# Norm statistics as full-width products with a stationary of ones, and the root and reciprocal on 512 columns

## The reference

```
def rmsnorm(x, g):
    xf = x.astype(jnp.float32)
    y = xf * lax.rsqrt(jnp.mean(xf * xf, axis=-1, keepdims=True) + EPS) * g.astype(jnp.float32)
    return y.astype(x.dtype)

def layer_norm(x, w, b, eps=LN_EPS):
    xf = x.astype(jnp.float32)
    mu = jnp.mean(xf, axis=-1, keepdims=True)
    var = jnp.mean(jnp.square(xf - mu), axis=-1, keepdims=True)
    y = (xf - mu) * lax.rsqrt(var + eps)
    return (y * w.astype(jnp.float32) + b.astype(jnp.float32)).astype(x.dtype)

def first_block(x, ...):
    u = rmsnorm(h, norm_mix_pre[l])
    z = u @ w_in[l]
    ...
    h = h + rmsnorm(m @ w_out[l], norm_mix_post[l])
    u2 = rmsnorm(h, norm_mlp_pre[l])
    a = jnp.square(jax.nn.relu(u2 @ w_up[l]))
    h = h + rmsnorm(a @ w_down[l], norm_mlp_post[l])

def second_block(x, c, ...):
    h = rms_norm(x, norm_mix_w[i]) * (1.0 + scale) + shift
    x = x + gate * mixer_sublayer(h, ...)
    h = rms_norm(x, norm_ffn_w[i]) * (1.0 + scale) + shift
    x = x + gate * ffn_sublayer(h, w_ffn_in[i], w_ffn_down[i])
    return rms_norm(x, final_norm_w)
```

## Time and profile before

| | us |
|---|---|
| median of three runs (lowest, highest) | 1763.21 (1762.67, 1766.19) |
| the profiled execution | 1764.47 |
| its span | 1762.7 |
| TensorE busy | 1714.2 (97%) |
| VectorE busy | 870.5 (49%) |
| ScalarE busy | 688.9 (39%) |
| GpSimd busy | 820.1 (47%) |

### The profile page before, as it was taken

The page is one execution under the profiler, slowest core; times in us unless marked ns, Lnnn a source line. Parts: engine busy times, 40 slices in busy tenths (PEclk is TensorE's granted clock), DMA queues, the critical chain, the costliest instruction groups (busy, mean ns, idle before and its releaser), DMA issues.

```text
span 1762.7 us, 22062 instructions
## 1 busy us (share of the span) xinstructions
PE 1714.2 (97%) x7994; PEld 1389.4 (79%) x7994; DVE 870.5 (49%) x1262; ACT 688.9 (39%) x933; POOL 820.1 (47%) x615
## 2 busy tenths in 40 slices
PE   7999999899999999899999999999999999999997
PEld 4777778678888888677888888778888788888886
DVE  4333464481817177588787878862544311101112
ACT  4333364421212123446465564684423322222231
POOL 4343354444546465443434434344455344664453
PEclk9999999899999999899999999999999899999998
DMA  4222222262534452142332232212223122332232
GB/s 180 72 72 73 93 75 93 81 228 109 195 139 178 155 178 96 51 143 96 107 109 95 95 119 95 96 67 101 94 74 115 59 98 101 128 120 95 95 120 95
DMA packets 30199, 193.26 MB, mean 110 GB/s; under 512 B 3360, under 2 KB 3360, under 8 KB 11328
## 3 DMA queue, kind: packets, MB, share of 16 engines
q1 hardware_dynamic: 23184, 158.89, 25.0%
q10 hardware_dynamic: 6960, 33.62, 5.7%
HBM read 190.34 MB, written 2.16 MB: 109 GB/s over the span
## 4 chain that ended last, share of the span: by engine, by line
PE 79%; issue 10%; POOL 7%; DVE 2%; ACT 2%; DMA 1%; POOLq 0%; DVEq 0%; SPq 0%; ACTq 0%
PE gemm_bank L465 19%; PE gemm_bank L458 19%; PE gemm_bank L459 18%; POOL w_lo L421 7%; PE gemm_bank L512 5%; PE gemm_bank L496 5%; PE gemm_bank L505 3%; PE gemm_bank L500 2%; PE aux_bank L815 1%; ACT w_hi L1000 1%; PE aux_bank L564 1%; PE aux_bank L820 1%; PE aux_bank L800 1%; DMA w_raw<-weights_dram 1%; PE aux_bank L590 1%
## 5 line engine op out<-in xcount | busy, mean ns | idle before, releaser
L421 POOL TENSOR_TENSOR w_lo<-w_raw,w_hi 128x512 fp32r<-128x512 f32 x588 | 795.0, 1383 | 911.8 <-ACT w_hi L1000 911.8
L458 PE MATMUL gemm_bank<-a_hi,w_hi 128*128 128x512 f32 x1216 | 486.3, 400 | 1.4 <-ACT w_hi L1000 1.4
L459 PE MATMUL gemm_bank<-a_lo,w_hi 128*128 128x512 f32 x1216 | 476.2, 392 | 0.0
L1000 ACT ACTIVATE w_hi<-w_raw 128x2048 fp32r<-128x2048 f32 x147 | 280.2, 1906 | 186.1 <-PE gemm_bank L465 138.8
L465 PE MATMUL gemm_bank<-a_hi,w_lo 128*128 128x512 f32 x1216 | 307.2, 395 | 2.7 <-POOL w_lo L421 2.7
L458 PEld LDWEIGHTS gemm_bank<-a_hi,w_hi 128*128 128x128 f32 x1216 | 229.8, 189 | 53.6 <-issue 4.8
L465 PEld LDWEIGHTS gemm_bank<-a_hi,w_lo 128*128 128x128 f32 x1216 | 226.6, 188 | 56.3 <-issue 5.5
L459 PEld LDWEIGHTS gemm_bank<-a_lo,w_hi 128*128 128x128 f32 x1216 | 229.8, 189 | 48.1 <-issue 1.9
L1788 DVE SCALAR_TENSOR_TENSOR aux_bank<-scratch,gcol,aux_bank 128x511 f32<-128x511 f32 (+15 forms) x240 | 165.9, 735 | 15.0 <-ACT aux_bank L1199 12.7
L458 PE MATMUL gemm_bank<-b_hi,w_hi 128*128 128x512 f32 x368 | 144.8, 394 | 0.0
L459 PE MATMUL gemm_bank<-b_lo,w_hi 128*128 128x512 f32 x368 | 143.4, 390 | 0.0
(11 more groups left out here) (327 smaller groups left out, 2099.6 us busy)
## 6 DMA issues: line engine op xcount, KB each, us to landing
w_raw<-weights_dram SPq DMA_DIRECT2D x147, 1024.0 KB, 4.7
arena<-ada_dram ACTq DMA_DIRECT2D x32, 768.0 KB, 4.3
acc<-cum_rows ACTq DMA_DIRECT2D x8, 512.0 KB, 3.8
...
```

Of the source, the lines that this page charges most:

```text
L421: ins = pool.tensor_tensor(wlo[s][:, w], raw[s][:, w], whi[s][:, w].bitcast(F32), ALU.subtract)
L458: pe.matmul(gemm_bank[bank][:, :], whi[slot][:, w], hi[:, k, :], start=(n == 0), stop=False)
L459: pe.matmul(gemm_bank[bank][:, :], whi[slot][:, w], lo[:, k, :], start=False, stop=False)
L1000: act.activation(whi[panel % 2][:, :], raw[panel % 2][:, :], ACT.Copy).then_inc(w_hi_ready, 1)
```

## The change

Five places get another form: the first norm, the residual of the first block, the convolution's layer norm (mean and variance), the norm before the FFN, and the final norm. The operands change roles. The 128x128 matrix of ones is stationary and the 128x512 sum moves, so that one product gives the sum over channels of every token, already repeated on all 128 partitions, as a 128x512 bank. `row_root` takes the root of the whole bank into `r_row`, `row_inverse` the reciprocal of all 512 columns into `aux[1]` (into `r_row` itself at the first norm). The spreading products and the copy of the first norm go; the mean is folded into a fused centering on VectorE.

At the residual, only seven squares are added on VectorE; the eighth is summed by a second product. The norms before the MLP and between the blocks, and the sums by groups of the scan's output, are as before.

```
 
+            def first_sums():
+
+                pe.wait_ge(sq_ready, KC)
+                pe.wait_ge(added[0], 6)
+                pe.matmul(aux[0][:, :], ones[:, :], sq[:, 1, :], start=True, stop=False)
+                pe.matmul(aux[0][:, :], ones[:, :], sq_acc, start=False, stop=True).then_inc(sum_done, 1)
...
                 if first:
-                    sums(0)
+                    first_sums()
                 tile_high(i, 1, 2, 4, 8, wide(2), a_hi, a_lo, first=True)
-                if first:
-                    spread(0)
                 tile_low(i, 1, 2, 4, wide(2), a_hi, first=True)
...
-            def sums_of_sum(steps, squares_made=None):
+            def row_sums(steps, squares_made):
 
                 pe.wait_ge(sq_sum_step, steps)
-                parts = [sq_sum]
-                if squares_made is not None:
-                    pe.wait_ge(ysq_ready, squares_made)
-                    parts.append(sq[:, 1, :])
-                for n, of in enumerate(parts):
-                    for j in range(QT):
-                        mm = pe.matmul(aux[0][:, j:j + 1], of[:, j * P:(j + 1) * P], ones[:, 0:1],
-                                       start=(n == 0 and j == 0), stop=(n == len(parts) - 1 and j == QT - 1),
-                                       skip_group_check=True)
-                mm.then_inc(sum_done, 1)
-
-            sums_of_sum(9)
-            spread(1)
+                pe.matmul(aux[0][:, :], ones[:, :], sq_sum, start=True, stop=False)
+                pe.wait_ge(ysq_ready, squares_made)
+                pe.matmul(aux[0][:, :], ones[:, :], sq[:, 1, :], start=False, stop=True).then_inc(sum_done, 1)
+
+            row_sums(8, 8)
...
-            def token_sums(parts, signal):
-                for n, of in enumerate(parts):
-                    for j in range(QT):
-                        mm = pe.matmul(aux[0][:, j:j + 1], of[:, j * P:(j + 1) * P], ones[:, 0:1],
-                                       start=(n == 0 and j == 0), stop=(n == len(parts) - 1 and j == QT - 1),
-                                       skip_group_check=True)
-                mm.then_inc(signal, 1)
-
             gate_tile(0)
             pe.wait_ge(u_sum_step, KC)
             pe.wait_ge(uc_ready, KC)
-            token_sums((u_sum,), mean_done)
-            gate_tile(1, (0,))
-            pe.wait_ge(mean_ready, 1)
-            for j in range(QT):
-                mm = pe.matmul(aux[1][:, j * P:(j + 1) * P], neg_mean[:, j:j + 1].to_broadcast([P, P]), ident[:, :],
-                               start=True, stop=True)
-            mm.then_inc(mean_spread, 1)
-            gate_tile(1, (1, 2))
+            pe.matmul(aux[1][:, :], ones[:, :], u_sum, start=True, stop=True).then_inc(mean_spread, 1)
+            gate_tile(1)
             gate_tile(2)
+            pe.wait_ge(ln_low_step, 3)
+            pe.matmul(aux[0][:, :], ones[:, :], ln_sq[:, 0, :], start=True, stop=False)
             pe.wait_ge(ln_sum_step, 3)
-            pe.wait_ge(ln_low_step, 3)
-            token_sums((ln_sq[:, 0, :], ln_sum), sum_done)
-            gate_tile(3, (0,))
-            spread(5)
-            gate_tile(3, (1, 2))
+            pe.matmul(aux[0][:, :], ones[:, :], ln_sum, start=False, stop=True).then_inc(sum_done, 1)
+            gate_tile(3)
...
-            spread(6)
+            row_sums(25, 24)
...
+            def row_root(n, e=0):
+                act.wait_ge(sum_done, n + 1)
+                act.activation(r_row, aux[0][:, :], ACT.Sqrt, bias=eps[:, e:e + 1], scale=1.0 / D).then_inc(root_ready, 1)
...
-            roots(0, sum_done, 1)
+            row_root(0)
...
-            roots(5, sum_done, 6, e=1)
+            row_root(5, e=1)
...
+            def row_inverse(n, dst):
+                dve.wait_ge(root_ready, n + 1)
+                dve.reciprocal(dst, r_row).then_inc(r_ready, 1)
+                dve.wait_ge(r_ready, n + 1)
+                dve.sem_inc(rinv_ready, 1)
+
             def normed_shifted(n, q, base, part):
 
-                inverse(n)
-                dve.wait_ge(r_ready, n + 1)
+                row_inverse(n, aux[1][:, :])
                 for k in range(KC):
                     dve.scalar_tensor_tensor(a_raw[:, k, :], h[:, k, :],
                                              gain2[:, KC * part + k:KC * part + k + 1], aux[1][:, :],
...
-                inverse(n)
-                dve.wait_ge(r_ready, n + 1)
+                row_inverse(n, aux[1][:, :])
                 dve.wait_ge(a_lo_ready, a_used)
...
-            root_row(0)
+            row_inverse(0, r_row)
+            dve.sem_inc(r_row_ready, 1)
...
             dve.memset(sq_sum, 0.0).then_inc(sq_sum_step, 1)
-            with dve.Fori(0, 2) as i:
-                for j in range(4):
-                    dve.wait_ge(ysq_ready, 4 * i + j + 1)
-                    dve.wait_ge(sq_sum_step, 4 * i + j + 1)
-                    dve.tensor_tensor(sq_sum, sq_sum, sq[:, j % 2, :], ALU.add).then_inc(sq_sum_step, 1)
+            for k in range(KC - 1):
+                dve.wait_ge(ysq_ready, k + 1)
+                dve.wait_ge(sq_sum_step, k + 1)
+                dve.tensor_tensor(sq_sum, sq_sum, sq[:, k % 2, :], ALU.add).then_inc(sq_sum_step, 1)
+            dve.wait_ge(sq_sum_step, KC)
+            dve.sem_inc(sq_sum_step, 1)
...
-            dve.wait_ge(mean_done, 1)
-            dve.tensor_scalar(neg_mean[:, :], aux[0][:, 0:QT], -1.0 / D, None, ALU.mult).then_inc(mean_ready, 1)
             dve.wait_ge(mean_spread, 1)
             for k in range(KC + 2):
                 if k < KC:
-                    dve.tensor_tensor(conv_u[:, k, :], conv_u[:, k, :], aux[1][:, :], ALU.add).then_inc(centered, 1)
+                    dve.scalar_tensor_tensor(conv_u[:, k, :], aux[1][:, :], -1.0 / D, conv_u[:, k, :],
+                                             ALU.mult, ALU.add).then_inc(centered, 1)
...
-            inverse(5)
-            dve.wait_ge(r_ready, 6)
             dve.wait_ge(centered, KC)
+            row_inverse(5, aux[1][:, :])
             dve.wait_ge(yz_ready, 4 * GROUPS)
...
-            inverse(7)
-            dve.wait_ge(r_ready, 8)
+            row_inverse(7, aux[1][:, :])
```

13 lines of the change are left out of this document (4 added, 9 removed).

## The result

The changed kernel takes 1765.82 us (median of 20 runs, 1764.52 to 1767.55), the kernel before 1761.94 in the same session (20 runs, 1760.46 to 1766.29). The ratio is 1.0018, with a 95% interval of 1.0012 to 1.0024: slower by 3.2 us, between 2.1 and 4.2. The forecast was +4.35 us and 1767.6. Direction and mechanism were right; the difference of the medians is 3.9. Of the 1.8 us by which the time itself is under the forecast, 1.3 belong to the starting point: the three runs shown of before had a median of 1763.21, the twenty of the comparison 1761.94.

What follows compares the result with a forecast made beforehand. TensorE, busy 97% of the span, was taken as the bound, with chain length deciding at the norms; -1.2 + 1.6 + 0 + 1.0 + 1.45 + 1.5 = +4.35 us gave 1767.6 us, range 1764.0 to 1771.0.

Steps and rivals of the forecast that it cites:

- What bounds the kernel: Whole kernel: TensorE is busy 97% of the span; at each changed norm only the length of the chain counts.
- The reciprocal: VectorE at all five places: 512 columns take 3.36 us, from the slope of narrower rows; +3.2 us in each chain.
- Rivals two: Five reciprocals: each is dearer, 3.82 us, adding 2.3 us to the sum, 1769.9 us; chance 0.12.
- three: Five reciprocals: 9.3 ns a column, up to 4.9 us each, adding 7.7 us, 1775.3 us; chance 0.06.
- four: Five reciprocals: divides overlap, 0.69 us each, so the change gains 7.9 us, 1755.3 us; chance 0.07.
- First norm: First norm: scores begin earlier, the long reciprocal being covered by the third tile; -1.2 us.
- Residual: Residual of the first block: sums end 0.75 us earlier, but the first scaled chunk comes later; +1.6 us.
- Layer norm: Convolution's layer norm: 0 us for the chain through ScalarE, +1.0 us because TensorE idles and its clock falls.
- FFN norm: Norm before the FFN: clock falls during the sums, scaling starts later; +1.45 us, +2.2 if the clock holds.
- final norm: Final norm: the same chain with nothing behind it, scaling starts later; +1.5 us, 2.2 with a warm clock.
- The sum: All five places together: +4.35 us, forecast 1767.6 us from the median of the runs shown.
- Rival one: Layer norm clock doesn't fall (0), FFN norm gives half back (+0.7): +2.6 us in all, 1765.8, no change; chance 0.22.

Runs made afterwards that it cites:

- Experiment 1: Changed kernel with its five wide reciprocals cut to the first 4 of 512 columns, the rest left out; 1753.41 us, ratio 0.9947 to the kernel before.

## Why the prediction was right, step by step

**What bounds the kernel.** Right. TensorE got 10.4 us less work and the kernel got slower; only the chain at each norm counted.

**The reciprocal.** Right to 0.01 us: 3.36 by the line through the 16- and 128-column rows, 3.353 to 3.362 measured. Rivals two (3.82), three (up to 4.9) and four (0.69) fell with that row. The estimate from the Trainium skill (VectorE: DVE Perf Modes, "First, the fixed hardware budget"), 4.27 us from a repeat count of 8, is 27% too high here: 3.36 us for 512 columns is 6.56 ns a column with everything in, and the slope 6.3. Where a trace has two sizes of the same instruction, the line through them was the better source. Experiment 1 shows that this instruction carries the whole loss.

**First norm, -1.2.** Measured -1.00 at the site, -1.6 (-3.2 to 0) by the run of it alone. The row was ready 6.06 us after the first sum, where the working has 6.0; the step from there to the scores took 1.86 us and not the 1.67 carried over from the earlier trace rows.

**Residual, +1.6.** Against the profile used, 4.39, the site came out at +1.75; against the mean of eight profiles, 4.75, at +1.4; the run of it alone gave +2.3 (+0.9 to +3.9).

**Layer norm, 0 for the chain and +1.0 for the clock.** The chain: the mean 1.4 earlier, as forecast, the variance 1.68 later, +0.28 in all; the fused centering costs 0.16 of this, where up to 0.5 was allowed (the pitch of 0.67 us taken for it did not come: the eight take 4.86 us, the plain ones took 4.87). The clock: it fell, as forecast, in all three profiles that have this norm wide with the reciprocal, and stayed low for 3.4 to over 6 us; that costs 0.2 to 1.4 us soon after, mean 0.9, and 0 to 1.2, mean 0.7, by the FFN norm. The changed kernel's own profile is the mildest of the three. So +1.0 stands as a size that other executions show and this profile does not.

**FFN norm, +1.45, and final norm, +1.5.** The sizes are right, +1.37 and +1.45 against the mean of ten profiles, and the run of the two alone gave +2.8 for 2.95. But the working behind them has a flaw. It took the low clock of the profile over to the changed kernel, reckoned the wide sums at half speed, and so expected the FFN scaling some 1.45 us after where the same profile had it. In fact the wide form came out at 7.28 us, hardly more than the 7.14 of that profile, since the clock held for it; and the narrow form, on other executions, takes 4.9 to 7.15. The profile shown of before was one of the long ones at both places (7.14 and 6.75, means 5.91 and 5.80): 2.2 us above the mean, which is nearly all of the 2.5 us by which it lay above the median of its kernel, and most of why the pair of profiles differs by 0.3 us only. Two errors cancelled, and that was luck: both forms were put too late by the same low clock. Against the narrow form at its fastest (4.91 and 4.77) the wide one costs 2.4 and 2.5 us, near the +2.2 that the prediction gave for a clock that holds.

**The sum, +4.35.** By sites -1.00 + 1.4 + 0.28 + 0.9 + 1.37 + 1.45 = +4.4, or +4.2 with the low clock's cost taken at the FFN norm. By the runs of the parts -1.6 + 2.3 + 0.2 + 2.8 = +3.7. By the ratio +3.2 (2.1 to 4.2), by the medians +3.9. The forecast is thus just above the upper end of the interval of the ratio, and no term can be named that is wrong by more than the measurements allow. Rival one (+2.6) lies within that interval; what it assumed, that the clock would not fall at the layer norm, did not happen, but in the changed kernel's profile the fall cost nothing by the FFN norm. The two cannot be told apart by the time. What stays open is why the mean alone gained 3.2 us for 1.25 at its site.
